# Regrouping the gated convolution's weights and starting its taps tile pair by tile pair, in a two-block transformer kernel

## The chip, the cores and the metric

The kernel runs on one core of one Trainium2 chip. TensorE (PE) multiplies, VectorE (DVE) and ScalarE (ACT) prepare its operands and take its results, SyncE issues the weight transfers. The metric is the device time in microseconds of one execution, as the median of three.

## What is computed

Two blocks over a sequence of 256 tokens with 2048 channels, all in float32. The first block (attention with a recurrence, then an MLP) is not touched. The second has two layers of this form, and the change is in these:

```python
z = h @ w_in[l]
q_lat, kv_lat, k_rope, mla_gate, conv_in, conv_gate = jnp.split(z, splits, axis=-1)   # 512, 256, 64, 1024, 2048, 1024
q = (rms_norm(q_lat, q_lat_g[l]) @ w_q_up[l]).reshape(b, s, N_HEADS, QK_DIM)
kv = (rms_norm(kv_lat, kv_lat_g[l]) @ w_kv_up[l])
...   # attention over 8 heads
mla_out = attn * jax.nn.silu(mla_gate)
u_val, u_gate = jnp.split(conv_in + glu_b[l], 2, axis=-1)
u = u_val * jax.nn.sigmoid(u_gate)                       # 1024 channels
u = causal_depthwise_conv(u, dw_w[l], dw_b[l])           # 31 taps per channel
u = jax.nn.silu(layer_norm(u, conv_ln_g[l], conv_ln_b[l]))
conv_out = (u @ w_pw[l] + b_pw[l]) * jax.nn.silu(conv_gate)
y = jnp.concatenate([mla_out, conv_out], axis=-1) @ w_out[l]
x = x + gate * y
```

## The kernel before

**Weights.** A float32 product is made of three products of rounded parts: high x high, high x low, low x high. Weights come from memory into four raw buffers (RAW). They are cut in *halves*, pieces of at most 1024 columns; for each half ACT writes the high part (WH, line 1922), DVE subtracts and writes the low part (WL, line 1084, called a split here), and PE multiplies both. There are four buffers of each part (`NHL = 4`), so ACT can make the high part of half j only when PE has finished half j - 4 (a wait on the semaphore `half_done`), and a DVE that is behind has at most that reserve before PE waits for it.

**Groups.** The weight columns are taken in groups, in an order written out by hand in `weight_course`. In a layer: 512 gates of the convolution (channel tiles 0 to 3), 256 + 256 of its values, 384 columns of key and value latents, 512 of query latents, the up-projection of the key and value latents (`w_kv_up`, four groups of one half), the other 512 gates, the other 512 values, the up-projection of the query latents (`w_q_up`, three groups of two halves), the gates of the attention (2 x 512) and of the convolution's output (4 x 256), then the halves of `w_out2` and `w_pw`. The two layers have the same program. I number the halves of a layer from 0: the first gates are halves 0 to 7, the query latents 24 to 31, the second gates 36 to 43, the second values 44 to 51, `w_q_up` 52 to 57.

**Two forms of product.** `products` multiplies each 128-column tile of weights in three matmuls of 256 columns (lines 578 to 580). `joint_products` is used for groups in `LAYER_JOINT`: the high weights go once against high and low hidden state side by side (512 columns, line 630), and the low weights against the high state (256 columns, line 632); ACT then takes the second half of the PSUM bank and DVE adds the first.

**PSUM pairs.** Each group is summed in a pair of PSUM banks. Groups in one pair follow each other: `n.before` is the mark (semaphore and value) that says that the pair's last group was taken out, and PE waits for it before the next group's first matmul:

```python
        if n.before:
            pe.wait_ge(*n.before)
```

For the second values of the convolution the mark is `taken`. DVE gives it after `glued` has taken the values out of PSUM, added the bias and multiplied by the gates (line 1820, four instructions of 256 columns, UV<-PS,PK,UG).

**Strands.** Everything else (normalisation, heads, attention, convolution) is written as generators, one per engine, and each is moved on by one step, a *beat*, behind each half. After a beat `cut_ahead` issues the next split, that of half j + 4 behind half j. So each engine's order is fixed: body of half j, beat j, split of half j + 4. `begin` hands out the halves; what stands in its loop body comes ahead of the beat. The convolution's taps are such a strand: tap 0 of a channel tile is an ACT instruction (line 2142), taps 1 to 30 are DVE instructions (line 1443, UG<-UV,PK,UG), 4 in a beat, 3 in the first `SLOW_TURNS` = 20. The first four channel tiles start behind half 15, the other four behind half 51. `channel_norm` starts when both are through.

Of the kernel before, what the change touches and what calls it, by code (L numbers as in the profile page):

```python
# [28 lines left out]
GLU_VALUES, GLU_GATES, Q_LATENT, KV_LATENT, MLA_GATES, CONV_GATES = ((0, 1), 5), (2, 6), 3, 4, (7, 8), (9, 10, 11, 12)  # L29
LAYER_JOINT = GLU_VALUES[0] + CONV_GATES  # L30
# [70 lines left out]
def weight_groups():  # L101

    return {
        "w_in": (16, [256] * 13 + [512] * 2 + [256] * 4),
        "w_out": (16, [512] * 4),
        "w_up": (16, [256] * 32),
        "w_down": (32, [512] * 8),
        "w_in2": (16, [256] * 2 + [512] * 2 + [384] + [512] * 4 + [256] * 4),
        "w_q_up": (4, [512] * 3),
        "w_kv_up": (2, [512] * 4),  # L110
        "w_pw": (8, [512] * 2),
        "w_out2": (16, [512] * 4),
    }
# [41 lines left out]
class Course:  # L155
# [84 lines left out]
def weight_course(t):  # L240
# [111 lines left out]
    "n_sum n_part n_mean n_sub n_sq n_ss n_ms n_root n_scale n_silu p_h p_l pw g_mm g_col g_out g_row g_mul x2"  # L352
# [124 lines left out]
def tensor_program(e, m, signals, plan):  # L477
# [451 lines left out]
    def channel_norm(L, taps):  # L929
# [3 lines left out]
        for n in range(15):  # L933
            if n == 0:
                b = small()
                pe.wait_ge("taps0", 124 * L + 124)
                pe.wait_ge("taps1", 124 * L + 124)
                spread_sum(b, lambda i: UG[:, i, :]).then_inc(signals["n_sum"], 1)
                free[b] = ("n_part", 2 * L + 1)
# [77 lines left out]
    for L in range(2):  # L1017
# [6 lines left out]
        products(group[f"w_in2_{L}", GLU_GATES[0]], *hidden, h, cols=4, early=h_early(2 + L))  # L1024
        course.pace = 99
        for g in GLU_VALUES[0]:
            joint_products(group[f"w_in2_{L}", g], h)
        taps = [course.start(convolution(L, 0))]
        products(group[f"w_in2_{L}", KV_LATENT], *hidden, h, cols=3)
        side_k = course.start(key_latents(L))  # L1030
        products(group[f"w_in2_{L}", Q_LATENT], *hidden, h, cols=4)
# [17 lines left out]
        for g in CONV_GATES:  # L1049
            joint_products(group[f"w_in2_{L}", g], h)  # L1050
        mla = tile_of("OH"), tile_of("OL"), lambda kt: ("o_l", 4 * L + kt // 2 + 1)
# [16 lines left out]
def vector_program(e, m, signals, plan):  # L1068
# [365 lines left out]
    def convolution(L, c0):  # L1434
        UV, UG = m["UV"], m["UG"]
        dw = pk(f"dw_w{L}").rearrange("p (c j) -> p c j", j=31)
        name = f"taps{c0 // 4}"
        for turn_ in course.tap_steps(L, c0):
            for n in turn_:
                j, c = n // 4, c0 + n % 4  # L1440
                if j:
                    dve.wait_ge(name, 124 * L + n - 3)
                    e.scalar_tensor_tensor(UG[:, c, :], UV[:, c, j:j + 256], dw[:, c, j:j + 1], UG[:, c, :], ALU.mult,  # L1443
                                           ALU.add).then_inc(signals[name], 1)
# [133 lines left out]
    def channel_norm(L, taps):  # L1578
# [3 lines left out]
        for n in range(15):  # L1582
            if n in (0, 2, 6, 8):
# [197 lines left out]
    for L in range(2):  # L1781
# [23 lines left out]
        def gated(c0):  # L1805

            dve.wait_ge(*group[f"w_in2_{L}", GLU_GATES[0]].taken)
            dve.wait_ge("joint_sum", 2 * joint_index(c0 // 2, L) + 2)
            tt("glu", UV[:, c0:c0 + 2, 30:286], UV[:, c0:c0 + 2, 30:286], UG[:, c0:c0 + 2, :], ALU.mult)

        def glued(g, c0):
            n = group[f"w_in2_{L}", g]
            for j, _ in course.begin(n):
                if j < n.done - 1:
                    continue
                dve.wait_ge("half_done", n.done)
                dve.wait_ge("uz", L + 1)
                dve.wait_ge(*group[f"w_in2_{L}", GLU_GATES[1]].taken)
                for f in range(4):
                    op = e.scalar_tensor_tensor(m["UV"][:, c0 + f, 30:286],  # L1820
                                                bank[2 * n.pair + f // 2][:, 256 * (f % 2):256 * (f % 2) + 256],
                                                pk(f"glu_b{L}")[:, c0 + f:c0 + f + 1], m["UG"][:, c0 + f, :], ALU.add,
                                                ALU.mult)
                op.then_inc(signals["taken"], 1)

        course.pace = 1
        course.group(group[f"w_in2_{L}", GLU_GATES[0]])
        course.pace = 99
        a, b = GLU_VALUES[0]
        course.group(group[f"w_in2_{L}", a])  # L1830
        n = group[f"w_in2_{L}", b]
        for j, _ in course.begin(n):
            if j == n.first + 1:
                summed(a, UV[:, 0:2, 30:286])
                gated(0)
            if j == n.done - 1:
                summed(b, UV[:, 2:4, 30:286])
                gated(2)
        taps = [course.start(convolution(L, 0))]
        course.group(group[f"w_in2_{L}", KV_LATENT])  # L1840
        side_k = course.start(key_latents(L))
        course.group(group[f"w_in2_{L}", Q_LATENT])
# [6 lines left out]
        course.group(group[f"w_in2_{L}", GLU_GATES[1]])  # L1849
        glued(GLU_VALUES[1], 4)  # L1850
        taps.append(course.start(convolution(L, 4)))
        norm = course.start(channel_norm(L, taps))
        course.drain(side_q)
        for g in range(3):
            course.group(group[f"w_q_up_{L}", g])
        flags.add(("queries", L))
        before = None
        for n in [group[f"w_in2_{L}", g] for g in MLA_GATES + CONV_GATES] + [
# [5 lines left out]
            before = next((g for g in CONV_GATES if group[f"w_in2_{L}", g] is n), None)  # L1864
        course.drain(side, norm)
# [44 lines left out]
def scalar_program(e, m, signals, plan, t):  # L1910
# [222 lines left out]
    def convolution(L, c0):  # L2133
        UV, UG = m["UV"], m["UG"]
        dw = pk(f"dw_w{L}").rearrange("p (c j) -> p c j", j=31)
        for turn_ in course.tap_steps(L, c0):
            for c in range(c0, c0 + 4) if turn_[0] == 0 else ():
                if c0:
                    act.wait_ge(*group[f"w_in2_{L}", GLU_VALUES[1]].taken)
                else:  # L2140
                    act.wait_ge("glu", 2 * L + c // 2 + 1)
                e.activation(UG[:, c, :], UV[:, c, 0:256], ACT.Identity, scale=dw[:, c, 0:1],
                             bias=pk(f"dw_b{L}")[:, c:c + 1]).then_inc(signals[f"taps{c0 // 4}"], 1)
# [20 lines left out]
    def query_latents(L):  # L2164
        QL, R2 = m["QN"][:, 0:4, :], m["R2"]
        for n in range(6):
            if n == 0:
                act.wait_ge(*group[f"w_in2_{L}", Q_LATENT].taken)
# [94 lines left out]
    def channel_norm(L, taps):  # L2263
# [3 lines left out]
        for n in range(15):  # L2267
            if n == 1:
# [46 lines left out]
    def store_R(n, dst):  # L2315
# [3 lines left out]
        op.then_inc(signals["stored"], 1)  # L2319

    def store_biased(n, dst, func, bias):
        act.wait_ge("half_done", n.done)
        for f in range(4):
            op = e.activation(dst(f), bank[2 * n.pair + f // 2][:, 256 * (f % 2):256 * (f % 2) + 256], func,
                              bias=bias[:, f:f + 1])
# [224 lines left out]
    for L in range(2):  # L2550
# [9 lines left out]
        def conv_gate(g, f0):  # L2560
            n = group[f"w_in2_{L}", g]
            course.group(n)
            store_biased(n, lambda f: UG[:, f0 + f, :], ACT.Sigmoid, glu[:, 8 + f0:12 + f0])
# [10 lines left out]
        conv_gate(GLU_GATES[0], 0)  # L2574
        course.pace = 99
        for c0, g in zip((0, 2), GLU_VALUES[0]):
            n = group[f"w_in2_{L}", g]
            for j, _ in course.begin(n):
                if j == n.done - 1:
# [241 lines left out]
```

## Time and profile before

| | |
|---|---|
| time, median of 3 (lowest to highest) | 1962.79 us (1962.68 to 1963.76) |
| the profiled execution's own time | 1963.59 us |
| its span, first to last instruction | 1961.8 us |
| PE busy | 1939.5 us, 99% |
| DVE busy | 1525.5 us, 78% |
| ACT busy | 1069.1 us, 54% |
| granted TensorE clock | 1.000 |

The two layers stand at about 1135 to 1541 us and 1545 us to the end of the span. A busy share says how long an engine had something to do, and not whether what it did was what the next one waited for; that is read from the waits and from the order of the instructions in time.

### The profile page before, as it was taken

The numbers are of one execution on the slowest core, as the hardware profiler recorded it, in microseconds if no ns is written. First come the engines' busy times: TensorE is split into PE (matmuls) and PEld (weight loads), VectorE is DVE, ScalarE is ACT, GpSimd is POOL, SyncE is SP. The second block draws the span as 40 slices with busy tenths as digits, with TensorE's granted clock in tenths as the row PEclk, the third lists the DMA queues.
The fourth block names the chain that finished last, engine by engine and source line by source line (L and its number), as shares of the span: only waits on it lengthen the run. The fifth ranks groups of instructions, "written<-read, shape, count | busy, mean of one in ns | idle before, by whom it ended". The sixth has DMA issues, their size and how long they took to land.

```text
span 1961.8 us, 27925 instructions
## 1 busy us (share of the span) xinstructions
PE 1939.5 (99%) x11546; PEld 1683.0 (86%) x11546; DVE 1525.5 (78%) x2092; ACT 1069.1 (54%) x1545; POOL 0.2 (0%) x4
## 2 busy tenths in 40 slices
PE   7999999999999999999999999999999999999999
PEld 6888888888888888888888889999888899998887
DVE  6587776868887777888877567999966669999764
ACT  5474766465664433555543475554764566456742
POOL 0000000000000000000000000000000000000000
PEclk9999999999999999999999999999999999999999
DMA  7443445938889888989898734544455455454453
GB/s 283 153 164 124 139 151 200 358 134 296 332 337 335 331 332 331 340 321 338 330 334 331 254 125 165 187 168 139 163 188 181 147 193 173 151 172 135 172 194 123
DMA packets 63982, 442.59 MB, mean 226 GB/s; under 512 B 7248, under 2 KB 7536, under 8 KB 12400
## 3 DMA queue, kind: packets, MB, share of 16 engines
q1 hardware_dynamic: 61920, 434.30, 61.9%
q10 hardware_dynamic: 1936, 6.51, 1.0%
q8 instruction: 91, 1.49, 0.3%
q14 instruction: 35, 0.29, 0.0%
HBM read 438.67 MB, written 2.11 MB: 225 GB/s over the span
## 4 chain that ended last, share of the span: by engine, by line
PE 96%; DVE 2%; ACT 1%; DMA 0%; issue 0%; ACTq 0%; DVEq 0%
PE PS L630 22%; PE PS L632 11%; PE PS L509 11%; PE PS L511 11%; PE PS L510 11%; PE PS L578 7%; PE PS L579 7%; PE PS L580 7%; PE PS L501 6%; PE PS L657 1%; DMA X<-in_x 0%; DVE WL L1084 0%; DVE Y L1126 0%; ACT S L1985 0%; ACT WH L1922 0%
## 5 line engine op out<-in xcount | busy, mean ns | idle before, releaser
L1922 ACT ACTIVATE WH<-RAW 128x1024 fp32r<-128x1024 f32 (+1 forms) x636 | 663.6, 1049 | 752.3 <-PE PS L511 282.5
L1084 DVE TENSOR_TENSOR WL<-RAW,WH 128x1024 fp32r<-128x1024 f32 (+1 forms) x636 | 766.4, 1209 | 374.7 <-ACT WH L1922 373.4
L630 PE MATMUL PS<-HT,WH 128*128 128x512 f32 x1912 | 678.5, 398 | 0.0
L632 PE MATMUL PS<-HT,WL 128*128 128x256 f32 x1912 | 535.8, 280 | 0.0
L630 PEld LDWEIGHTS PS<-HT,WH 128*128 128x128 f32 x1912 | 358.6, 188 | 88.8 <-issue 7.2
L632 PEld LDWEIGHTS PS<-HT,WL 128*128 128x128 f32 x1912 | 361.3, 189 | 0.1
L578 PE MATMUL PS<-HT,WH 128*128 128x256 f32 x1008 | 291.2, 289 | 0.7 <-DVE HT L1135 0.4
L580 PE MATMUL PS<-HT,WL 128*128 128x256 f32 x1008 | 285.5, 283 | 0.0
L579 PE MATMUL PS<-HT,WH 128*128 128x256 f32 x1008 | 285.5, 283 | 0.0
L1093 DVE SCALAR_TENSOR_TENSOR RAW<-RAW,CB 128x2048 f32<-128x2048 f32 x96 | 219.3, 2284 | 0.0
L511 PE MATMUL PS<-WH,Ul 128*128 128x512 f32 x512 | 203.0, 396 | 0.0
L509 PE MATMUL PS<-WH,Uh 128*128 128x512 f32 x512 | 202.5, 396 | 0.0
L578 PEld LDWEIGHTS PS<-HT,WH 128*128 128x128 f32 x1008 | 193.4, 192 | 10.6 <-issue 7.8
L510 PE MATMUL PS<-WL,Uh 128*128 128x512 f32 x512 | 201.2, 393 | 0.0
L1443 DVE SCALAR_TENSOR_TENSOR UG<-UV,PK,UG 128x256 f32<-128x256 f32 x480 | 200.4, 478 | 0.2
L579 PEld LDWEIGHTS PS<-HT,WH 128*128 128x128 f32 x1008 | 193.6, 192 | 0.4
L580 PEld LDWEIGHTS PS<-HT,WL 128*128 128x128 f32 x1008 | 193.5, 192 | 0.0
L510 PEld LDWEIGHTS PS<-WL,Uh 128*128 128x128 f32 x512 | 96.1, 188 | 23.8
L511 PEld LDWEIGHTS PS<-WH,Ul 128*128 128x128 f32 x512 | 96.1, 188 | 23.7
L509 PEld LDWEIGHTS PS<-WH,Uh 128*128 128x128 f32 x512 | 96.1, 188 | 22.5
L509 PE MATMUL PS<-WH,HT 128*128 128x512 f32 x256 | 100.8, 394 | 0.0
L511 PE MATMUL PS<-WH,HT 128*128 128x512 f32 x256 | 99.8, 390 | 0.0
(317 smaller groups left out, 2026.7 us busy)
## 6 DMA issues: line engine op xcount, KB each, us to landing
RAW<-in_w_in SPq DMA_DIRECT2D x112, 1024.0 KB, 4.8
RAW<-in_ada_w SPq DMA_DIRECT2D x96, 1024.0 KB, 6.3
RAW<-in_w_up SPq DMA_DIRECT2D x64, 1024.0 KB, 5.8
RAW<-in_w_down SPq DMA_DIRECT2D x64, 1024.0 KB, 5.7
RAW<-in_w_out SPq DMA_DIRECT2D x48, 1024.0 KB, 4.8
RAW<-in_w_pw SPq DMA_DIRECT2D x8, 1024.0 KB, 4.8
RAW<-in_w_in SPq DMA_DIRECT2D x8, 768.0 KB, 4.2
RAW<-in_w_q_up SPq DMA_DIRECT2D x6, 1024.0 KB, 4.8
```

The costliest lines, as they stand in the source:

```text
L509: e.matmul(out, sh, mh, start=st, stop=False, skip_group_check=True)
L510: e.matmul(out, sh, ml, start=False, stop=False, skip_group_check=True)
L511: return e.matmul(out, sl, mh, start=False, stop=final, skip_group_check=True)
L578: e.matmul(out, sh, ah, start=first and i % 2 == 0, stop=False, skip_group_check=True)
L579: e.matmul(out, sh, al, start=False, stop=False, skip_group_check=True)
L580: op = e.matmul(out, sl, ah, start=False, stop=final, skip_group_check=True)
L630: e.matmul(bk[i][:, 0:512], wh[:, at], m["HT"][:, kt, :, :].rearrange("p a t -> p (a t)"), start=kt == 0, stop=False, skip_group_check=True)
L632: op = e.matmul(bk[i][:, 0:256], wl[:, at], HTh[:, kt, :], start=False, stop=kt == n.kts - 1, skip_group_check=True)
L1084: e.tensor_tensor(m[f"WL{j % NHL}"][:, 0:nk * w], m[f"RAW{i % NRAW}"][:, k0 * w:(k0 + nk) * w], m[f"WH{j % NHL}"][:, 0:nk * w].bitcast(F32 ...
L1093: e.scalar_tensor_tensor(raw[:, :], raw[:, :], 1.0, m["CB"][:, :], ALU.mult, ALU.mult, accum_out=mod[:, k:k + 1]).then_inc(signals["ada"], 1)
L1443: e.scalar_tensor_tensor(UG[:, c, :], UV[:, c, j:j + 256], dw[:, c, j:j + 1], UG[:, c, :], ALU.mult, ALU.add).then_inc(signals[name], 1)
L1922: e.activation(m[f"WH{j % NHL}"][:, 0:nk * w], m[f"RAW{i % NRAW}"][:, k0 * w:(k0 + nk) * w], ACT.Copy).then_inc(signals["high"], 1)
```

## The change

The convolution's gates and values of the same two channel tiles now come in one weight group: of 512 columns, 256 gates and 256 values. There are three such groups (`GLU`, for tiles 0 and 1, 4 and 5, 6 and 7), multiplied by `products`; tiles 2 and 3 come in two groups of 256 (`GLU_JOINT`, gates then values), multiplied by `joint_products`. The query latents are two groups of 256 with `joint_products`. The number of halves in a layer and their places stay the same. The taps start behind half 7 and behind half 43, and first only on one pair of channel tiles; the other pair joins in at a later turn. The multiplication by the gates is done pair by pair. The last steps of `channel_norm` wait for a flag that is set when all of `w_in2` has been multiplied.

```diff
-GLU_VALUES, GLU_GATES, Q_LATENT, KV_LATENT, MLA_GATES, CONV_GATES = ((0, 1), 5), (2, 6), 3, 4, (7, 8), (9, 10, 11, 12)
-LAYER_JOINT = GLU_VALUES[0] + CONV_GATES
+GLU, GLU_JOINT, Q_LATENT, KV_LATENT, MLA_GATES, CONV_GATES = (0, 6, 7), (1, 2), (3, 4), 5, (8, 9), (10, 11, 12, 13)
+LAYER_JOINT = GLU_JOINT + Q_LATENT + CONV_GATES
...
     def tap_steps(self, L, c0):
-        yield range(4)
-        n, turn = 4, 0
-        while n < 124:
-            k = min(3 if c0 == 0 and turn < SLOW_TURNS else 4, 124 - n)
-            yield range(n, n + k)
-            n, turn = n + k, turn + 1
+        later = 7 if c0 == 0 else 10
+        done = [0] * 4
+        for turn in range(99):
+            taps = []
+            if turn in (1, later):
+                taps = [(0, c0 + c) for c in ((0, 1) if turn == 1 else (2, 3))]
+            for _ in range(3 if c0 == 0 and later < turn <= later + SLOW_TURNS else 4):
+                c = min(range(4 if turn > later else 2), key=lambda c: done[c])
+                if turn > 1 and done[c] < 30:
+                    done[c] += 1
+                    taps.append((done[c], c0 + c))
+            yield taps
+            if sum(done) == 120:
+                return
...
-        weights(f"w_in2_{layer}", (GLU_GATES[0], *GLU_VALUES[0], KV_LATENT, Q_LATENT))
+        weights(f"w_in2_{layer}", (GLU[0], *GLU_JOINT, KV_LATENT, *Q_LATENT))
         weights(f"w_kv_up_{layer}", range(4))
-        weights(f"w_in2_{layer}", (GLU_GATES[1], GLU_VALUES[1]))
+        weights(f"w_in2_{layer}", GLU[1:])
...
-            elif tensor[:4] == "w_pw" or tensor[:5] == "w_in2" and g == GLU_VALUES[1]:
+            elif tensor[:4] == "w_pw" or tensor[:5] == "w_in2" and g in GLU:
                 taken += 1
                 mark = ("taken", taken)
```

In PE's program:

```diff
-        for g in (GLU_GATES[1], GLU_VALUES[1]):
-            products(group[f"w_in2_{L}", g], *hidden, h, cols=4)
+        products(group[f"w_in2_{L}", GLU[1]], *hidden, h, cols=4)
         taps.append(course.start(convolution(L, 4)))
+        products(group[f"w_in2_{L}", GLU[2]], *hidden, h, cols=4)
```

In DVE's program:

```diff
+        def glued(g, c0, gates):
             n = group[f"w_in2_{L}", g]
+            dve.wait_ge("half_done", n.done)
+            dve.wait_ge("uz", L + 1)
+            dve.wait_ge("u_sig", 4 * L + gates)
+            for c in range(c0, c0 + 2):
+                op = e.scalar_tensor_tensor(UV[:, c, 30:286], bank[2 * n.pair + 1][:, 256 * (c - c0):256 * (c - c0) + 256],
+                                            pk(f"glu_b{L}")[:, c:c + 1], UG[:, c, :], ALU.add, ALU.mult)
+            op.then_inc(signals["taken"], 1)
...
-        course.group(group[f"w_in2_{L}", GLU_GATES[1]])
-        glued(GLU_VALUES[1], 4)
+        course.group(group[f"w_in2_{L}", GLU[1]])
         taps.append(course.start(convolution(L, 4)))
+        n = group[f"w_in2_{L}", GLU[2]]
+        for j, _ in course.begin(n):
+            if j == n.first + 1:
+                glued(GLU[1], 4, 3)
         norm = course.start(channel_norm(L, taps))
         course.drain(side_q)
         for g in range(3):
-            course.group(group[f"w_q_up_{L}", g])
+            n = group[f"w_q_up_{L}", g]
+            for j, _ in course.begin(n):
+                if g == 0 and j == n.first + 1:
+                    glued(GLU[2], 6, 4)
```

In ACT's program, tap 0 of a channel tile:

```diff
-            for c in range(c0, c0 + 4) if turn_[0] == 0 else ():
-                if c0:
-                    act.wait_ge(*group[f"w_in2_{L}", GLU_VALUES[1]].taken)
+            for j, c in turn_:
+                if j:
+                    continue
+                if c in (2, 3):
+                    act.wait_ge("glu", L + 1)
                 else:
-                    act.wait_ge("glu", 2 * L + c // 2 + 1)
+                    act.wait_ge(*group[f"w_in2_{L}", GLU[(c + 2) // 4 if c else 0]].taken)
```

**DVE around `w_q_up`, layer 0.** L1084 (before) and L1097 (changed) are the splits, L1443 and L1462 the taps, L1820 and L1839 the multiplication of PSUM values by the gates, whose last instruction gives `taken`. Before, from the split of half 53:

```order
L1084 TENSOR_TENSOR WL<-RAW,WH 128x1024 [waits high]
L1443 SCALAR_TENSOR_TENSOR UG<-UV,PK,UG 128x256 [waits taps0] x4
L1084 TENSOR_TENSOR WL<-RAW,WH 128x1024 [waits high]
L1820 SCALAR_TENSOR_TENSOR UV<-PS,PK,UG 128x256 [waits stored,uz,half_done]
L1820 SCALAR_TENSOR_TENSOR UV<-PS,PK,UG 128x256 x3
L1443 SCALAR_TENSOR_TENSOR UG<-UV,PK,UG 128x256 [waits taps0] x4
L1084 TENSOR_TENSOR WL<-RAW,WH 128x1024 [waits high] x2
L1443 SCALAR_TENSOR_TENSOR UG<-UV,PK,UG 128x256 [waits taps1] x4
```

In the changed kernel, from the same split:

```order
L1097 TENSOR_TENSOR WL<-RAW,WH 128x1024 [waits high]
L1462 SCALAR_TENSOR_TENSOR UG<-UV,PK,UG 128x256 [waits taps1] x4
L1097 TENSOR_TENSOR WL<-RAW,WH 128x1024 [waits high]
L1462 SCALAR_TENSOR_TENSOR UG<-UV,PK,UG 128x256 [waits taps1] x4
L1097 TENSOR_TENSOR WL<-RAW,WH 128x1024 [waits high]
L1462 SCALAR_TENSOR_TENSOR UG<-UV,PK,UG 128x256 [waits taps1] x4
L1097 TENSOR_TENSOR WL<-RAW,WH 128x1024 [waits high]
L1839 SCALAR_TENSOR_TENSOR UV<-PS,PK,UG 128x256 [waits u_sig,half_done]
L1839 SCALAR_TENSOR_TENSOR UV<-PS,PK,UG 128x256
L1462 SCALAR_TENSOR_TENSOR UG<-UV,PK,UG 128x256 [waits taps1] x4
```

The instructions that give `taken` stood behind the split of half 54 and now stand behind that of half 56, with two more splits and eight taps ahead of them; there are two of them in place of four (two others moved ahead, into the body of half 45).

**PE at the second group of `w_q_up`.** QLh and QLl are the query latents' parts. Before:

```order
L578 MATMUL PS<-QLh,WH 128x256
L579 MATMUL PS<-QLl,WH 128x256
L580 MATMUL PS<-QLh,WL 128x256
L578 MATMUL PS<-QLh,WH 128x256 [waits split,taken]
L579 MATMUL PS<-QLl,WH 128x256
```

In the changed kernel:

```order
L587 MATMUL PS<-QLh,WH 128x256
L588 MATMUL PS<-QLl,WH 128x256
L589 MATMUL PS<-QLh,WL 128x256
L587 MATMUL PS<-QLh,WH 128x256 [waits split,taken]
L588 MATMUL PS<-QLl,WH 128x256
```

The wait stands at the same place, the first matmul of half 54, and for the same mark; what has to be done on DVE before the mark is given has moved, as shown above.

## Rows read from the trace of the kernel before

**Rows 1.** The page, busy time of each engine and the clock by slices.

```profile
PE 1939.5 (99%) x11546; PEld 1683.0 (86%) x11546; DVE 1525.5 (78%) x2092; ACT 1069.1 (54%) x1545; POOL 0.2 (0%) x4
...
PEclk9999999999999999999999999999999999999999
```

**Rows 2.** Waits of PE over the whole span: us in total, times, longest.

```profile
PE PS L657 <- DVE Y L1126: 14.0, 3, 12.3
PE PS L501 <- DVE Y L1080: 1.6, 1, 1.6
PE PS L564 <- ACT VT L1965: 1.5, 2, 0.9
```

**Rows 3.** Windows: length, busy time of PE, PEld, DVE, ACT, POOL, then clock.

```profile
12.30:18.20 5.90, 5.65 (x24) 4.93 (x24) 5.88 (x14) 3.75 (x9) 0.00 (x0) 1.00 1.01 361
...
1160.00:1541.00 381.00, 381.00 (x2604) 343.92 (x2603) 313.04 (x519) 215.08 (x314) 0.00 (x0) 1.00 0.50 171
...
1565.00:1957.00 392.00, 392.00 (x2669) 353.66 (x2668) 317.07 (x523) 213.63 (x306) 0.00 (x0) 1.00 0.49 166
```

**Rows 4.** PE's timeline, a plain group and a joint group: start, us, instruction.

```profile
1200.16 0.28 PE L578 MATMUL PS<-HT,WH 128*128 128x256 f32 x1
...
1201.60 0.28 PE L578 MATMUL PS<-HT,WH 128*128 128x256 f32 x1
...
1189.20 0.39 PE L630 MATMUL PS<-HT,WH 128*128 128x512 f32 x1
...
1190.24 0.39 PE L630 MATMUL PS<-HT,WH 128*128 128x512 f32 x1
```

**Rows 5.** PE's timeline, first matmul of half 52 and of half 54; half 52, layer 1.

```profile
1300.69 0.28 PE L578 MATMUL PS<-QLh,WH 128*128 128x256 f32 x1
...
1306.45 0.28 PE L578 MATMUL PS<-QLh,WH 128*128 128x256 f32 x1
...
1709.41 0.28 PE L578 MATMUL PS<-QLh,WH 128*128 128x256 f32 x1
```

**Rows 6.** DVE's timeline, splits of halves 53 to 56, in brackets idle before.

```profile
1298.49 1.67 DVE L1443 SCALAR_TENSOR_TENSOR UG<-UV,PK,UG 128x256 f32<-128x256 f32 x4
1300.08 1.22 DVE L1084 TENSOR_TENSOR WL<-RAW,WH 128x1024 fp32r<-128x1024 f32 x1
1301.21 1.67 DVE L1443 SCALAR_TENSOR_TENSOR UG<-UV,PK,UG 128x256 f32<-128x256 f32 x4
1302.80 1.22 DVE L1084 TENSOR_TENSOR WL<-RAW,WH 128x1024 fp32r<-128x1024 f32 x1
1304.05 1.66 DVE L1820 SCALAR_TENSOR_TENSOR UV<-PS,PK,UG 128x256 f32<-128x256 f32 x4
1305.62 1.67 DVE L1443 SCALAR_TENSOR_TENSOR UG<-UV,PK,UG 128x256 f32<-128x256 f32 x4
```

**Rows 7.** The same, layer 1.

```profile
1712.77 1.66 DVE L1820 SCALAR_TENSOR_TENSOR UV<-PS,PK,UG 128x256 f32<-128x256 f32 x4
```

**Rows 8.** DVE's timeline before that: last wait, and splits of halves 48 and 49.

```profile
1267.12 1.23 DVE L1084 TENSOR_TENSOR WL<-RAW,WH 128x1024 fp32r<-128x1024 f32 x1 [0.32 <-ACT WH L1922]
...
1283.14 1.23 DVE L1084 TENSOR_TENSOR WL<-RAW,WH 128x1024 fp32r<-128x1024 f32 x1
1284.29 1.67 DVE L1443 SCALAR_TENSOR_TENSOR UG<-UV,PK,UG 128x256 f32<-128x256 f32 x4
1285.99 0.75 DVE L1525 SCALAR_TENSOR_TENSOR KN<-KN,PK,PS 128x512 f32<-128x512 f32 x1
1286.65 0.84 DVE L1528 TENSOR_TENSOR KP<-KV,PS 64x256 f32<-64x256 f32 x2
1287.53 1.23 DVE L1084 TENSOR_TENSOR WL<-RAW,WH 128x1024 fp32r<-128x1024 f32 x1
```

**Rows 9.** ACT's timeline: a high part, tap 0 of four tiles, two high parts.

```profile
1300.89 1.06 ACT L1922 ACTIVATE WH<-RAW 128x1024 fp32r<-128x1024 f32 x1 [1.76 <-PE PS L580]
1305.74 2.08 ACT L2142 ACTIVATE UG<-UV,PK 128x256 f32<-128x256 f32 x4 [3.79 <-DVE UV L1820]
1307.73 1.99 ACT L1922 ACTIVATE WH<-RAW 128x1024 fp32r<-128x1024 f32 x2
```

**Rows 10.** DVE's timeline, key and value latents: DVE without a wait.

```profile
1198.56 0.96 DVE L1084 TENSOR_TENSOR WL<-RAW,WH 128x768 fp32r<-128x768 f32 x1 [1.41 <-ACT WH L1922]
1199.44 1.27 DVE L1443 SCALAR_TENSOR_TENSOR UG<-UV,PK,UG 128x256 f32<-128x256 f32 x3
1200.63 0.95 DVE L1084 TENSOR_TENSOR WL<-RAW,WH 128x768 fp32r<-128x768 f32 x1
```

More of the change, by code:

```diff
@@ L1437, in convolution @@
         name = f"taps{c0 // 4}"
+        n, last = 120 * L, {}
         for turn_ in course.tap_steps(L, c0):
[L1439 to L1444, printed above, removed]
+            for j, c in turn_:
+                if not j:
+                    continue
+                if j == 1:
+                    dve.wait_ge("taps_a", 8 * L + c + 1)
+                else:
+                    dve.wait_ge(name, last[c])
+                n += 1
+                last[c] = n
+                e.scalar_tensor_tensor(UG[:, c, :], UV[:, c, j:j + 256], dw[:, c, j:j + 1], UG[:, c, :], ALU.mult,
+                                       ALU.add).then_inc(signals[name], 1)
             yield
@@ L1582, in channel_norm @@
         for n in range(15):
+            while n == 10 and ("inputs", L) not in flags:
+                yield
             if n in (0, 2, 6, 8):
@@ L1803, in summed, with gated @@
                 tt("joint_sum", part[:, i, :], bank[2 * n.pair + i][:, 0:256], part[:, i, :], ALU.add)
[L1805 to L1811, printed above, removed]
-            n = group[f"w_in2_{L}", g]
[L1813 to L1824, printed above, removed]
+        def gated():
+            dve.wait_ge("u_sig", 4 * L + 2)
+            dve.wait_ge("joint_sum", 2 * joint_index(GLU_JOINT[1], L) + 2)
+            tt("glu", UV[:, 2:4, 30:286], UV[:, 2:4, 30:286], UG[:, 2:4, :], ALU.mult)
@@ L1826, in vector_program @@
         course.pace = 1
-        course.group(group[f"w_in2_{L}", GLU_GATES[0]])
+        course.group(group[f"w_in2_{L}", GLU[0]])
         course.pace = 99
-        a, b = GLU_VALUES[0]
+        taps = [course.start(convolution(L, 0))]
+        a, b = GLU_JOINT
+        n = group[f"w_in2_{L}", a]
+        for j, _ in course.begin(n):
+            if j == n.first + 1:
+                glued(GLU[0], 0, 1)
+        n = group[f"w_in2_{L}", b]
+        for j, _ in course.begin(n):
+            if j == n.first + 1:
+                summed(a, UG[:, 2:4, :])
+            if j == n.done - 1:
+                summed(b, UV[:, 2:4, 30:286])
+                gated()
@@ L1830, in vector_program @@
+        course.group(group[f"w_in2_{L}", KV_LATENT])
+        side_k = course.start(key_latents(L))
+        a, b = Q_LATENT
         course.group(group[f"w_in2_{L}", a])
@@ L1833, in vector_program @@
             if j == n.first + 1:
-                summed(a, UV[:, 0:2, 30:286])
-                gated(0)
+                summed(a, m["QN"][:, 0:2, :])
             if j == n.done - 1:
[L1837 to L1842, printed above, removed]
+                summed(b, m["QN"][:, 2:4, :])
         side_q = course.start(query_latents(L))
@@ L2167, in query_latents @@
             if n == 0:
[L2168 removed]
+                act.wait_ge("joint_sum", 2 * joint_index(Q_LATENT[1], L) + 2)
                 act.wait_ge("l_ss", 2 * L + 1)
@@ L2267, in channel_norm @@
         for n in range(15):
+            while n == 10 and ("inputs", L) not in flags:
+                yield
             if n == 1:
@@ L2558, in scalar_program, with gate_pair @@
         glu = pk(f"glu_b{L}")
-        def conv_gate(g, f0):
+        def gate_pair(g, c0):
             n = group[f"w_in2_{L}", g]
-            course.group(n)
-            store_biased(n, lambda f: UG[:, f0 + f, :], ACT.Sigmoid, glu[:, 8 + f0:12 + f0])
+            act.wait_ge("half_done", n.done)
+            for c in range(c0, c0 + 2):
+                op = e.activation(UG[:, c, :], bank[2 * n.pair][:, 256 * (c - c0):256 * (c - c0) + 256], ACT.Sigmoid,
+                                  bias=glu[:, 8 + c:9 + c])
+            op.then_inc(signals["u_sig"], 1)
         def second_part(n, part, func=ACT.Copy, bias=None):
```

75 lines of the change are left out of this document (47 added, 28 removed).

## The prediction

> **What bounds the kernel now.** I start from the page: PE has something to do in 99% of the span and the granted clock is full in all slices [rows 1], so only two things can change the time: PE's own work, and a wait put in front of it. Then the waits of PE [rows 2]. There are three of any size, 12.3 us of the largest at the kernel's start and the rest at the borders between stages. Inside the layers there is none, and the windows say the same without inference: in the 381 us from 1160 to 1541 PE is busy for 381.00, in the 392 us from 1565 to 1957 for 392.00 [rows 3]. So nothing that makes DVE or ACT quicker in the layers can be worth anything, and starting the taps earlier, which moves work off the end of a layer, is worth nothing by itself. The question is only whether DVE still delivers in time. It is busy for 313.04 of those 381 us [rows 3], which is not an idle engine, and what matters is how far it is behind at each place where PE needs it.
>
> That is read from DVE's timeline. Its last wait before `w_q_up` is at 1267.12, on ACT [rows 8]. From there it has more to do per half than PE. A turn of four taps and a split take 2.72 us from start to start (1300.08 to 1302.80 [rows 6]); a half of PE takes 2.88 us (1300.69 to 1306.45 for two [rows 5]). With the heads' instructions a turn takes 4.39 us (1283.14 to 1287.53 [rows 8]). So DVE falls behind by about 1.5 us in each of several halves, and wins back only 0.16 us in each after. PE does not notice, since four halves of split weights lie in reserve. At 1302.80 DVE starts the split of half 54 [rows 6], which PE starts at 1306.45 [rows 5]: the split is ready at 1304.02, 2.4 us early, where the reserve at full depth would be some 6 us. DVE lags, harmlessly, because splits are asked for four halves ahead. A result that PE asks for one half ahead does not have this reserve.
>
> **The change part by part.**
>
> *Query latents with a joint operand.* In a plain group twelve matmuls take 1200.16 to 1201.60, 0.360 us for each three; in a joint group three pairs take 1189.20 to 1190.24, 0.347 us each [rows 4]. Three matmuls and one pair do the same work, a 128-column weight tile in one of 16 row tiles. Four such tiles by 16 are 64 units a layer: 64 x 0.013 = 0.83 us, 1.7 us in two layers. This is the whole change in PE's work. The gates and values of tiles 0 to 7 change places but not form: 512 of their columns were joint before and 512 are now.
>
> *DVE's and ACT's work.* The joint latents cost DVE four additions a layer; the gating loses one multiplication of 512 columns. The taps are the same 240 a layer. None is on PE's path while the reserve holds.
>
> *The wait that is moved.* In a layer the PSUM pair of `w_q_up`'s second group (half 54) is the one that held the convolution's last values, before and now, and PE waits there for `taken`. Before, DVE took these values in the body of half 51, behind the split of half 54: at 1304.05, four instructions, 1.66 us, over at 1305.71 [rows 6]. PE came at 1306.45 [rows 5]: early by 0.74 us, with nothing to spare for more. Now they are taken in the body of half 53, behind the split of half 56 (the order above). Step by step, from the split of half 54 at 1302.80:
> - two turns of four taps and a split, 2.72 us each [rows 6], bring DVE to the start of the split of half 56: 1308.24;
> - from a split to this gating, 1.25 us (1302.80 to 1304.05): 1309.49;
> - four gating instructions take 1.57 us to the next start and 1.66 to their end; so two take 0.39 + 0.48 = 0.87: over at 1310.36.
>
> PE is there at 1306.45. It waits 3.9 us. The joint latents bring PE there 0.8 us sooner, but DVE as well, whose splits follow PE through `half_done` up to 1267.12; I count that gain once, above.
>
> Does DVE reach 1302.80 earlier than before? The turn behind half 44 is the same four taps, that behind half 45 has no tap (-1.59 us), and two gating instructions come ahead of it (+0.79): 0.8 us less. But tap 0 of two tiles is now done by ACT in that turn and waits for this gating. The split of half 48 ends at 1284.37 [rows 8], the gating at 1285.24, two tap-0 instructions take half of 2.08 us [rows 9], the high part of half 49 takes 1.06: 1287.34, and the split of half 49, at 1287.53 before, can start at about 1287.4. Of the 0.8 us some 0.1 stays. I take 3.8 us; if all of the 0.8 stayed it would be 3.1, and with a longer chain through ACT 4.2.
>
> The second layer is the same program: half 52 starts there at 1709.41 and the gating at 1712.77 [rows 5, 7], both 408.72 us after the first, so it waits as long: 7.6 us in two layers. What is queued behind the wait on PE is all the rest of the layer, and since PE waits for nothing else in it, there is no idle time later in which this comes back. ACT's tap 0 of tiles 6 and 7 waits for the same mark, with the high part of half 58 behind it; PE reaches that half four halves later, so it costs nothing. DVE, in return, is no longer behind after the stall, which no one needs.
>
> *Small waits.* A joint half is 0.1 us shorter, and DVE gets 24 taps into halves 10 to 15, so chains between small matmuls and DVE are tighter. Nothing in the trace shows such a wait; between 0 and 0.4 us a layer, I take 0.1.
>
> **Sum.** 1963.59 (the profiled execution; span 1961.8) - 1.7 + 7.6 + 0.2 = 1969.7. That execution was 0.8 us above the median of the runs, 1962.79, so for the median: 1962.79 + 6.1 = **1968.9 us**. Its own range, from 3.1 to 4.2 a layer and 0 to 0.4 for small waits: 1967.3 to 1970.3.
>
> **The clock.** The largest pause of PE in the layers before is nil, and that before them under 2 us [rows 2], and the clock is granted in full throughout [rows 3]. A pause of 3.8 us is longer than any inside the span after the start, so no row says that the clock survives it. If it falls to the lower of its two levels (1.2 for 2.4 GHz), PE works at half speed for a time that no row gives; bounded by the pause itself it would be up to 3.8 us at half speed, 1.9 us lost for each stall. The Trainium skill ("TensorE: Matmul & The Clock Gate", the table on what matters for kernels) says that idle gaps between bursts put the clock back to its lower level; by it each of the two stalls would cost more than its own length. No run so far shows it.
>
> **The rivals.**
> - *The mark is given in time* (not slower). If DVE were not behind, the gating in half 53's body would still stand behind that half's predecessor split, and come 1.06 (high part) + 1.25 + 0.87 = 3.2 us after half 52's end at 1303.57, at 1306.75: a wait of 0.3 us. This needs DVE to have won back the 3.6 us by which it is behind. It decides from there: each us of lag on DVE is one on PE. Against it is that the same 2.72 us turns run through halves 46 to 53 in both. Time: 1962.79 - 1.7 + 0.6, 1961.7, within what tells from no change. Chance 0.06.
> - *Half of it*: the ACT chain spares more, or DVE's turns are shorter with other neighbours; 1.9 us a layer, 1965.1. Chance 0.06.
> - *The clock falls* in one or both pauses: 1970.8 or 1972.7. Chance 0.17.
> - *Splits late as well*: in the key and value latents PE has halves of 2.16 us and DVE three taps and a split in 2.07 (1198.56 to 1200.63 [rows 10]), so a delay from halves 8 to 15 stays. DVE's work there rises from none to 4 taps in six halves (2.72 of 2.78 us) and gating; it starts the stage 1 to 2 us later than before, against a reserve of over 3. If it fails, PE waits for another 1 us a layer: 1970.9. Chance 0.05.
> - The forecast itself: 0.66.
>
> **How the numbers follow.** A measurement of this kernel tells about 0.2%, 3.9 us, from no change. Slower by more than that: the forecast, the late splits and the clock, 0.88. The in-time case and the half of it are within: 0.12, of which I give 0.02 to faster, for a gain that I don't see (PE's work alone gives only 1.7 us). The range leaves out those two cases below and the fall of the clock in both pauses above: 1966.3 to 1971.5.
>
> **What would show it.** Right: a wait of PE at the first matmul of `w_q_up`'s second group, line 587, released by DVE's line 1839, two times, some 3.8 us each; PE's busy time in the layers otherwise 0.8 us less each; DVE without a pause for ACT from half 49 to the gating; joint pairs at 0.347 us in halves 24 to 31. Wrong: no such wait, or one under 2 us; a granted clock under 1 behind it; new waits for line 1097 in the key and value latents.

## The result and the profile after

The changed kernel takes 1973.97 us (median of 4, 1972.90 to 1974.22), the kernel before 1962.85: ratio 1.0054, 95% interval 1.0041 to 1.0066. It is slower, as forecast, but by 11.1 us in place of 6.1, and outside the range of 1966.3 to 1971.5.

The page of the changed kernel, span, busy times and the clock by slices, to be held against [rows 1]:

```profile
span 1971.1 us, 27683 instructions
PE 1940.2 (98%) x11418; PEld 1678.6 (85%) x11418; DVE 1528.8 (78%) x2102; ACT 1068.0 (54%) x1549; POOL 0.2 (0%) x4
...
PEclk9999999999999999999999999999999999999999
```

With 128 matmuls fewer PE has more busy time, and the page's clock row shows nothing, since a digit stands for 49 us. The line of the cores does: span and mean granted clock.

```profile
core 0: 1971.1 us, clock 0.998
```

The three largest waits of PE over the whole span (us in total, times, longest), against [rows 2]:

```profile
PE PS L666 <- DVE Y L1139: 14.0, 3, 12.3
PE PS L587 <- DVE UV L1839: 7.6, 2, 3.8
PE PS L510 <- DVE Y L1093: 1.6, 1, 1.6
```

The middle row is new, and it is the forecast one: first matmul of half 54, released by the gating, twice, 3.8 us each. DVE's timeline up to it, against [rows 6] (the split of half 54 is that at 1301.50):

```profile
1301.50 1.22 DVE L1097 TENSOR_TENSOR WL<-RAW,WH 128x1024 fp32r<-128x1024 f32 x1
1302.64 1.67 DVE L1462 SCALAR_TENSOR_TENSOR UG<-UV,PK,UG 128x256 f32<-128x256 f32 x4
1304.22 1.22 DVE L1097 TENSOR_TENSOR WL<-RAW,WH 128x1024 fp32r<-128x1024 f32 x1
1305.36 1.67 DVE L1462 SCALAR_TENSOR_TENSOR UG<-UV,PK,UG 128x256 f32<-128x256 f32 x4
1306.94 1.22 DVE L1097 TENSOR_TENSOR WL<-RAW,WH 128x1024 fp32r<-128x1024 f32 x1
1308.19 0.88 DVE L1839 SCALAR_TENSOR_TENSOR UV<-PS,PK,UG 128x256 f32<-128x256 f32 x2
```

The gating ends 1308.19 + 0.88 - 1301.50 = 7.57 us after the start of the split of half 54; the prediction had 1310.36 - 1302.80 = 7.56. Both PE and DVE come here 1.3 us earlier than before: 0.4 us of it is the joint latents, 0.9 us the first block, whose program is unchanged (see the last section). What the prediction left out of its likeliest case is what PE does next. PE's timeline at the wait:

```profile
1305.02 0.28 PE L589 MATMUL PS<-QLh,WL 128*128 128x256 f32 x1
1309.12 0.38 PE L587 MATMUL PS<-QLh,WH 128*128 128x256 f32 x1 [3.82 <-DVE UV L1839]
...
1309.60 0.41 PE L587 MATMUL PS<-QLh,WH 128*128 128x256 f32 x1
1309.81 0.41 PE L588 MATMUL PS<-QLl,WH 128*128 128x256 f32 x1
1310.02 0.41 PE L589 MATMUL PS<-QLh,WL 128*128 128x256 f32 x1
```

Behind the pause a matmul follows the last after 0.21 us, where it took 0.12 [rows 5]. The windows of the changed kernel (length, busy time of PE with its matmuls, PEld, DVE, ACT, POOL, then the granted clock) show why:

```profile
1297.00:1304.00 7.00, 7.00 (x61) 7.00 (x60) 7.00 (x15) 3.68 (x5) 0.00 (x0) 1.00 0.66 247
1304.00:1309.00 5.00, 1.31 (x11) 1.09 (x10) 4.97 (x10) 2.03 (x3) 0.00 (x0) 1.00 0.49 177
1309.00:1313.50 4.50, 4.38 (x24) 4.38 (x25) 4.37 (x10) 1.09 (x2) 0.00 (x0) 0.62 0.33 76
1313.50:1317.00 3.50, 3.50 (x32) 3.50 (x31) 2.07 (x4) 1.41 (x2) 0.00 (x0) 1.00 0.62 262
...
1723.00:1727.50 4.50, 4.50 (x26) 4.50 (x27) 4.24 (x9) 1.06 (x2) 0.00 (x0) 0.67 0.27 56
```

In the 4.5 us behind the pause the mean clock is 0.62, which is the lower level (1.2 GHz, half) for 0.38 / 0.5 x 4.5 = 3.4 us and the higher one for the rest; in layer 1 it is 0.67, so 3.0 us at the lower level lie in this window. PE counts as busy all the while.

### The profile page after: what moved, and what is told of

It reads as the page before. It is cut to its first block, busy times and chain, and to the rows that moved or that the text cites. A ratio compares the mean times of both kernels' runs of the same rounds, so it can differ in the third digit from the quotient of the medians.

```text
span 1971.1 us, 27683 instructions
## 1 busy us (share of the span) xinstructions
PE 1940.2 (98%) x11418; PEld 1678.6 (85%) x11418; DVE 1528.8 (78%) x2102; ACT 1068.0 (54%) x1549; POOL 0.2 (0%) x4
## 4 chain that ended last, share of the span: by engine, by line
PE 83%; DVE 14%; ACT 2%; issue 1%; DMA 0%; ACTq 0%; DVEq 0%
PE PS L639 22%; PE PS L520 11%; PE PS L518 11%; PE PS L519 11%; PE PS L641 11%; PE PS L510 5%; DVE UG L1462 5%; DVE WL L1097 5%; PE PS L587 4%; PE PS L588 4%; PE PS L589 4%; ACT WH L1956 1%; PE PS L666 1%; DMA X<-in_x 0%; DVE Y L1139 0%
## 5 line engine op out<-in xcount | busy, mean ns | idle before, releaser
L1097 DVE TENSOR_TENSOR WL<-RAW,WH 128x1024 fp32r<-128x1024 f32 (+1 forms) x636 | 766.3, 1209 | 383.7 <-ACT WH L1956 382.0
L639 PE MATMUL PS<-HT,WH 128*128 128x512 f32 x2040 | 723.2, 398 | 0.1
L639 PEld LDWEIGHTS PS<-HT,WH 128*128 128x128 f32 x2040 | 382.5, 188 | 95.2 <-issue 7.4
L587 PE MATMUL PS<-HT,WH 128*128 128x256 f32 x880 | 254.5, 289 | 1.6 <-DVE HT L1148 1.3
L588 PE MATMUL PS<-HT,WH 128*128 128x256 f32 x880 | 249.0, 283 | 0.0
L1462 DVE SCALAR_TENSOR_TENSOR UG<-UV,PK,UG 128x256 f32<-128x256 f32 x480 | 200.7, 479 | 0.3
L587 PEld LDWEIGHTS PS<-HT,WH 128*128 128x128 f32 x880 | 168.7, 192 | 11.2 <-issue 7.2
L588 PEld LDWEIGHTS PS<-HT,WH 128*128 128x128 f32 x880 | 169.0, 192 | 0.3
L518 PEld LDWEIGHTS PS<-WH,Uh 128*128 128x128 f32 x512 | 96.1, 188 | 22.5
```

Of the source, the lines that this page charges most:

```text
L518: e.matmul(out, sh, mh, start=st, stop=False, skip_group_check=True)
L587: e.matmul(out, sh, ah, start=first and i % 2 == 0, stop=False, skip_group_check=True)
L588: e.matmul(out, sh, al, start=False, stop=False, skip_group_check=True)
L639: e.matmul(bk[i][:, 0:512], wh[:, at], m["HT"][:, kt, :, :].rearrange("p a t -> p (a t)"), start=kt == 0, stop=False, skip_group_check=True)
L1097: e.tensor_tensor(m[f"WL{j % NHL}"][:, 0:nk * w], m[f"RAW{i % NRAW}"][:, k0 * w:(k0 + nk) * w], m[f"WH{j % NHL}"][:, 0:nk * w].bitcast(F32 ...
```

## The experiments

I call a stretch of 3.4 us at half clock a spell. One takes 3.4 x 0.5 / 1972 = 0.0009 off the mean clock of a whole execution, so 0.999, 0.998 and 0.997 are read as one, two and three spells. The traces show one (e4_move_alone) or two (the changed kernel, twice); three are read from a mean of 0.997 alone. Each run is compared with runs of the kernel before on the same chip (medians 1962.83 us for e1_early, e2_warm, e3_short and e4_move_alone, 1963.69 for a2_again, e5_fewer_taps, e6_joint_alone and e7_norm_late, 1962.90 for e8_joint_only).

To compare a stage between runs I use the first and last start of PE's matmuls on the query latents, line 578 or 587, `w_q_up`, halves 52 to 57. Before, they go from 1300.7 to 1317.6, 16.9 us.

**e1_early: the late gating put back by two halves, from the body of half 53 to that of half 51.** In DVE's program:

```diff
             if j == n.first + 1:
                 glued(GLU[1], 4, 3)
+            if j == n.done - 1:
+                glued(GLU[2], 6, 4)
...
-                if g == 0 and j == n.first + 1:
-                    glued(GLU[2], 6, 4)
```

In ACT's program:

```diff
-        course.group(group[f"w_in2_{L}", GLU[2]])
-        gate_pair(GLU[2], 6)
+        for j, _ in course.begin(group[f"w_in2_{L}", GLU[2]]):
+            if j == group[f"w_in2_{L}", GLU[2]].done - 1:
+                gate_pair(GLU[2], 6)
```

> The changed kernel with one thing moved: the last two gating instructions (tiles 6 and 7), which give the mark for the second group of w_q_up, stand in the body of half 51, on DVE and on ACT, in place of half 53. Theory (DVE's lag reaches PE through this mark alone, and the pause then lowers the clock): no wait for it, clock 1.000, only the joint latents are left, so 1.7 us under before: 1961.2 us. Rival (the time went to splits that come late because taps and gating lie in other halves): little changes, 1970 us or more. Rival (only the wait counts and the clock's fall is by chance): 1961 to 1963 as well, so this run does not tell it from the theory.

Measured: 1963.38 us, ratio 1.0002 (0.9993 to 1.0011), clock 1.000. The wait for line 1839 is gone from PE's waits; this one call, moved, takes away 10.6 us between the medians and 9.5 us between the spans of the profiled executions (1971.1 and 1961.6). But 1961.2 was expected, and of the gain by the joint latents nothing is to be seen. PE's timeline in the first group of query latents of this kernel, three pairs of the joint form:

```profile
1214.06 0.40 PE L639 MATMUL PS<-HT,WH 128*128 128x512 f32 x1
...
1215.12 0.40 PE L639 MATMUL PS<-HT,WH 128*128 128x512 f32 x1
```

1.06 us, 0.353 for a pair, where [rows 4] had 0.347 in halves 8 to 15 of the same form: half of the expected gain. And a wait that the kernel before does not have, in its waits of PE:

```profile
PE PS L510 <- DVE HS L1536: 0.4, 2, 0.2
```

**e2_warm: the wait filled with matmuls that nobody needs.**

```diff
         for g in range(3):
+            if g == 1:
+                keep_warm(16)
             products(group[f"w_q_up_{L}", g], tile_of("QLh"), tile_of("QLl"), lambda kt: ("l_l", 2 * L + 2), cols=4)
```

> The changed kernel with 16 matmuls of 128 columns on constants, whose results nobody uses, put on PE ahead of the wait at the second group of w_q_up. By the trace of before such a matmul takes 0.223 us, so they fill 3.6 of the 3.9 us. The wait's end is set by DVE and stays. Theory (a pause of PE lowers the clock for 3.4 us, which costs 1.4 us in each layer, seen in the profile): clock 1.000, span 2.8 us under the changed kernel's 1971.1, median 1969 to 1970. Rival (the low clock in the profile is not caused by the pause): clock stays 0.998, 1973 to 1974 us.

Measured: 1970.11 us (1970.03 to 1970.17), ratio 1.0036 (1.0024 to 1.0049), clock 1.000. The windows of this kernel at the same place:

```profile
1304.00:1309.00 5.00, 4.93 (x44) 4.74 (x42) 4.97 (x10) 2.03 (x3) 0.00 (x0) 1.00 0.53 172
1309.00:1313.50 4.50, 4.37 (x36) 4.38 (x37) 4.41 (x11) 2.15 (x3) 0.00 (x0) 1.00 0.30 78
```

The added matmuls fill the wait but for 0.2 us (the trace has two instructions for each of the 16):

```profile
1305.19 3.73 PE L510 MATMUL PS<-CN 128*128 128x128 f32 x32
1309.13 0.39 PE L587 MATMUL PS<-QLh,WH 128*128 128x256 f32 x1 [0.20 <-DVE UV L1841]
```

Behind the filled wait 36 matmuls fit into the 4.5 us, behind the empty one 24. The stage `w_q_up` takes from 1299.4 to 1320.4, 21.0 us, in the changed kernel 1299.4 to 1321.9, 22.5 us. So the pause itself costs 21.0 - 16.9 = 4.1 us and the clock 1.5 more. In layer 1 the same stage takes 16.9 us before, 20.9 here and 22.2 in the changed kernel: 4.0 for the pause, 1.3 for the clock. Together the clock costs 2.8 us in the profiled executions, which is also the difference of their spans, 1971.1 - 1968.3.

The medians are 3.9 us apart, 1.0 more. No trace shows where this 1.0 lies. A third spell does not explain it: of the changed kernel's four executions only the one at 1974.22 us had a mean clock of 0.997, while 1973.91 and 1974.04 had 0.998, like the profiled one at 1972.90. What fits is the first block, which takes 0.9 us more in some executions than in others (last section): it took the shorter time in both profiles, and the five executions of e2_warm lie within 0.1 us of its profiled one.

**e3_short: the late gating one half earlier.**

```diff
-                if g == 0 and j == n.first + 1:
+                if g == 0 and j == n.first:
                     glued(GLU[2], 6, 4)
```

> The changed kernel with the last gating moved one half ahead, from the body of half 53 to that of half 52. On DVE one turn of taps and split, 2.72 us, is no longer ahead of it. Theory: PE waits 3.8 - 2.7 = 1.1 us in each layer, the clock does not fall, so 1962.85 - 1.7 + 2.2 + 0.3 = 1963.7 us. Rival (any wait at this place lowers the clock): 2.8 us more, 1966.5 us.

Measured: 1964.71 us, ratio 1.0010 (1.0001 to 1.0019), clock 1.000. The wait, in its waits of PE:

```profile
PE PS L587 <- DVE UV L1839: 2.1, 2, 1.1
```

One turn of taps and split less ahead of the gating is 2.7 us less for PE to wait, and a pause of 1.1 us did not lower the clock in any of the eleven executions. The median is 1.0 us above the expectation, where the run with the early gating was 2.2 above: both counted 1.7 us for the joint latents, which bring only half of it (e8_joint_only below).

**e4_move_alone: the kernel before with only the gating of tiles 4 to 7 moved to the body of half 53.** The taps of these tiles and channel_norm start behind it.

```diff
-            for j, _ in course.begin(n):
-                if j < n.done - 1:
-                    continue
...
         for g in range(3):
-            course.group(group[f"w_q_up_{L}", g])
+            for j, _ in course.begin(group[f"w_q_up_{L}", g]):
+                if g == 0 and j == group[f"w_q_up_{L}", 0].first + 1:
+                    glued(GLU_VALUES[1], 4)
+            if g == 0:
+                taps.append(course.start(convolution(L, 4)))
+                norm = course.start(channel_norm(L, taps))
```

> The kernel before with one thing alone: its gating of tiles 4 to 7 is done in the body of half 53 in place of half 51, and the taps of these tiles start behind it. No joint latents, no regrouping, no early taps. Theory (the place of the mark on DVE's queue is the cause): DVE has a turn of taps less in between than the changed kernel, and four gating instructions, so the mark comes at 1309.5 in the time of before, PE waits 3.1 us in each layer; 1962.85 + 6.2 = 1969 us with the clock kept, 1971.9 if it falls in both. Rival (the regrouping and the early taps put DVE behind): no wait or one under 1 us, 1963 to 1965 us.

Measured: 1972.22 us (1970.62 to 1973.97), ratio 1.0049 (1.0035 to 1.0063). Without any of the regrouping almost the whole loss is there. Its waits of PE, and two of its windows behind the pause, layer 0 and layer 1:

```profile
PE PS L578 <- DVE UV L1818: 6.0, 2, 3.0
...
1309.00:1313.50 4.50, 4.50 (x39) 4.50 (x39) 1.25 (x2) 2.92 (x5) 0.00 (x0) 1.00 0.83 299
...
1717.00:1723.00 6.00, 3.00 (x17) 2.79 (x16) 4.79 (x7) 4.10 (x7) 0.00 (x0) 0.80 0.63 187
```

In this execution a pause of 3.0 us left the clock alone in layer 0 and lowered it in layer 1: a pause of that length can go either way. The five executions had mean clocks 0.999, 0.998, 0.998, 0.998, 0.997 and took 1970.62, 1971.85, 1972.27, 1972.22, 1973.97 us. Read as one, two and three spells, that is some 1.6 us each; only the first of them was traced.

**a2_again: the changed kernel once more.** No edit.

> The changed kernel as it is, once more, to see how the fall of the clock varies from one execution to the next. If each pause lowers the clock for one spell of 3.4 us, all runs lie at 1972.9 to 1974.2 with a mean clock of 0.998. If a pause can lower it for two spells, some runs show 0.997 or 0.996 and lie 1.5 us or more above the others. The waits themselves should not vary.

Measured: 1974.88 us (1973.10 to 1975.74), ratio 1.0055 (1.0043 to 1.0068). The clocks were 0.998, 0.998, 0.997, 0.998, 0.997 with 1973.2, 1973.1, 1975.1, 1975.74, 1974.88 us. The waits are again 7.6, 2, 3.8 in the profiled execution, the one at 1973.2 us with two spells. Two executions at 0.997 point to a third spell; neither was traced, so whether a third pause went with it isn't seen. One run at 0.998 took 1975.74, so not all of the spread is the clock's.

**e5_fewer_taps: seven taps less ahead of the late gating.**

```diff
-            for _ in range(3 if c0 == 0 and later < turn <= later + SLOW_TURNS else 4):
+            for _ in range(3 if c0 == 0 and later < turn <= later + SLOW_TURNS or c0 and turn <= 8 else 4):
```

> The changed kernel with three taps in place of four in turns 2 to 8 of the second convolution strand (behind halves 46 to 52), so 7 taps of 0.4 us less ahead of the late gating, made up by two more turns at the end. The mark stays where the change put it. Theory (the wait is as long as DVE's lag): the wait shrinks by 2.8 us to about 1.0 us in each layer, the clock stays, 1964.7 us as with the gating one half ahead. Rival (the wait is set by the place alone, by ACT's or PE's chain): still near 3.8 us and 1973 us.

Measured: 1965.58 us (1964.67 to 1967.70), ratio 1.0012 (1.0003 to 1.0021), clock 1.000. The mark stands where the change put it, and its row in the waits of PE is:

```profile
PE PS L587 <- DVE UV L1839: 2.1, 2, 1.0
```

The wait is DVE's lag: 2.8 us less work ahead of the gating, 2.8 us less wait. The eleven executions spread over 3.0 us at a full clock; the slower ones were not traced.

**e6_joint_alone: the query latents in the joint form, on the kernel before.** In this build the gates and values of channel tiles 4 to 7 are exchanged (the sizes and the work are the same), which the next run sets right.

```diff
-LAYER_JOINT = GLU_VALUES[0] + CONV_GATES
+LAYER_JOINT = GLU_VALUES[0] + Q_LATENT + CONV_GATES
...
-        products(group[f"w_in2_{L}", Q_LATENT], *hidden, h, cols=4)
+        for g in Q_LATENT:
+            joint_products(group[f"w_in2_{L}", g], h)
```

> The kernel before with the query latents in two groups with the joint form, and nothing else of the change. Forecast of the prediction: 1.7 us less, 1961.2 us. By the profiles of the changed kernel and of the one with early gating, where halves 24 to 31 took only 0.42 us less than before: 0.84 us less, 1962.0 us. If the small loss behind half 56 (0.7 us a layer) came with the joint latents and not with the earlier channel_norm, 1963.4 us.

Measured: 1962.88 us beside 1963.69 for the kernel before, ratio 0.9997 (0.9988 to 1.0006).

**e8_joint_only: the same with all of the computation in place.**

> The kernel before with the query latents in the joint form as its only change, all of the computation in place. By the run of the same form with gates and values of four channel tiles exchanged: halves 24 to 31 take 0.42 us less in each layer and nothing else moves, 0.85 us less in all, ratio 0.9996. Forecast of the prediction for this part: 1.7 us less, ratio 0.9991.

Measured: 1962.05 us beside 1962.90, 0.85 us less, ratio 0.9996 (0.9987 to 1.0005). That is the expectation by halves 24 to 31 and half of what the prediction had. It is the lowest median of the study, though the interval does not exclude no change.

**e7_norm_late: e1_early with channel_norm held back.** In all three programs:

```diff
         while any(strand in course.strands for strand in taps):
             yield
+        for _ in range(7):
+            yield
```

> The changed kernel with the early gating (1963.38 us), and channel_norm held back by seven turns, so that its steps fall on the halves on which they fell before. Theory (in that kernel halves 56 to 98 take 0.7 us a layer more than before, of which 0.4 because channel_norm's matmuls cut in at other places): 0.8 us less, 1962.5 us. Rival (the 0.4 comes from elsewhere): 1963.4 us.

Measured: 1963.51 us, ratio 0.9999 (0.9990 to 1.0008), on the chip whose median of before is 1963.69; e1_early was 0.55 us above its median of before, this one is 0.18 below. The profile tells it better, in the time from the first `w_q_up` matmul to the last start of a matmul on the attention's output (OH), half 97, in layer 0. The rows of e7_norm_late (duration min/median/max, then first and last start):

```profile
L587 PE MATMUL PS<-QLh,WH x48: 278/280/283, 1302.0 to 1318.9; 128*128 128x256 f32 x48
L518 PE MATMUL PS<-WH,OH x32: 392/397/582, 1438.2 to 1460.5; 128*128 128x512 f32 x32
```

and of e1_early:

```profile
L587 PE MATMUL PS<-QLh,WH x48: 278/280/283, 1299.5 to 1316.4; 128*128 128x256 f32 x48
L518 PE MATMUL PS<-WH,OH x32: 392/397/400, 1436.6 to 1458.4; 128*128 128x512 f32 x32
```

158.9 us in e1_early, 158.5 with channel_norm held back, and 158.2 both before (1300.7 to 1458.9) and in e8_joint_only (1299.6 to 1457.8). So an earlier channel_norm costs 0.4 us a layer, and 0.3 stay; the wait for the heads' reciprocal (HS), 0.2 in each layer, is most of that.

## Why the prediction was wrong

By its own steps:

- **What bounds the kernel**: right. PE was without a pause in the layers, so earlier taps brought nothing: e1_early, which has them without the wait, is 0.6 us above before.
- **The wait that is moved**: right in place, cause and size. 3.8 us forecast, 3.8 measured, in both layers. e3_short and e5_fewer_taps show that its length is DVE's lag (2.7 and 2.8 us less for one turn or seven taps less), e1_early that the place of the gating alone makes it, e4_move_alone that it needs nothing else of the change. Of the 0.8 us by which DVE might have come earlier nothing stayed, where 0.1 was forecast: it waited 0.69 us for ACT ahead of the split of half 49, at 1286.23, and from there to the gating for nothing. The stage loses 4.1 and 4.0 us by the pause, 0.2 to 0.3 more than the 3.8 of the sum.
- **Query latents with a joint operand**: right mechanism, twice too large. The term was 64 x 0.013 us a layer, from a pair at 0.347 us in halves 8 to 15. In halves 24 to 31 a pair takes 0.353, the term is 0.42 us a layer and 0.85 in all (e8_joint_only) in place of 1.7. I took the rate of the one place for that of the other.
- **Small waits**: 0.1 us a layer forecast, with 0.4 as the upper end. With the early gating it is 0.7 (e1_early), 0.4 of it from channel_norm's matmuls at other halves (e7_norm_late), which the prediction valued at nothing.
- **The clock**: this is the step that failed. The prediction put the clock's fall at nothing in its sum and kept it as a rival with a chance of 0.17. It wrote that "no row says that the clock survives it", and gave no reason for deciding that it does. In all nine executions of the changed kernel the mean clock was 0.998 or 0.997. e2_warm shows that the idle time of PE is the cause: with the mark given at the same time and PE kept at work, the clock stays, and the profiled execution is 2.8 us nearer to before (the median 3.9 us). The Trainium skill ("TensorE: Matmul & The Clock Gate", section "Why this matters for your kernels") says that idle gaps between matmul bursts throw the clock back to its lower level. The traces agree for the long pause: 0.62 of the clock behind 3.8 us, 1.00 behind 1.1, and either behind 3.0.
- **The price of the clock**: 1.9 us for each pause was the bound. A spell costs 1.5 us in layer 0 and 1.3 in layer 1 of the profiled executions. With both pauses the rival gave 1972.7 us; measured were 1973.97 and, on another chip, 1974.88 beside 1963.69.
- **A row that was misread**: the prediction says that the clock is granted in full throughout, by [rows 3]. The first window there has 1.00 as well, but 24 matmuls in 5.9 us where the next has 49. In the kernel before, PE's matmuls behind the idle 12.3 us at the start stand 0.21 us apart and last 0.41, as they do behind the pause here, and from 18.4 on they stand 0.12 apart:

```profile
14.99 0.41 PE L578 MATMUL PS<-HT,WH 128*128 128x256 f32 x1
15.21 0.41 PE L579 MATMUL PS<-HT,WH 128*128 128x256 f32 x1
...
18.82 0.28 PE L578 MATMUL PS<-HT,WH 128*128 128x256 f32 x1
18.93 0.28 PE L579 MATMUL PS<-HT,WH 128*128 128x256 f32 x1
```

So the column of the clock can't be trusted at the start of a span, and the one long idle stretch on record was followed by the lower pace. PE had done nothing before it, so it shows no fall; but it was the nearest row for a long pause, and it spoke for the rival.

The sum with the sizes as measured in the profiles: two pauses 4.1 + 4.0 = 8.1, clock 2.8, joint latents -0.85: 10.05 us. The spans differ by 1971.1 - 1961.8 = 9.3 us; but the profiled execution of the kernel before had the slower first block, by 0.9 us, which makes 10.2. The medians differ by 11.1. The 0.9 left over is the size of that same step of the first block, which would come in if most executions of the changed kernel had the slower one; there is no trace of them, so this is not shown.

The sum leaves nothing for channel_norm and the small waits, and the traces agree there. From the last `w_q_up` matmul on QLh in layer 0 to the first in layer 1 it is 391.6 us before, 391.8 in e1_early, but 391.2 in the changed kernel, e2_warm, e3_short and e5_fewer_taps; 0.4 less than before is what the joint latents of layer 1 bring. So where PE has waited for the gating, even for 1.1 us, the 0.7 us of e1_early are not lost. I take this for slack that DVE has after the wait; no run tests that reason.

What stays open: the last 0.9 us between the medians, whether and why a third spell comes in some executions, and why a pause of 3.0 us lowers the clock in one layer and not in the other. No run moved a pause of one length in time.

## What to carry to other kernels

When an instruction that frees a PSUM bank is moved past others on a busy engine, count from the engine's last idle moment to the new place, and compare with when PE comes: a result asked for one step ahead has none of the reserve that lets the same engine run late with work asked for four steps ahead. A pause of PE must be priced with the clock: ask whether it is longer than any the trace has survived, and if so put the fall into the likeliest sum. Read the clock also from the distance of equal matmuls, since its column can say 1.00 where they stand twice as far apart. If the pause can't be avoided, dummy matmuls in it give back the clock's part (here 2.8 us in the profiled executions), but moving the mark to an earlier place gives back nearly all of the loss (9.5 us).

## What the hardware showed unexpectedly

The joint form has two rates. A pair takes 0.347 us in some stretches and 0.353 in others. In the layers the place decides: halves 8 to 15 are fast and halves 24 to 31 slow in every profile. In the first block the same instructions go at either rate from one execution to the next; in the 40 us from 430 on, the row of line 632's matmuls in the kernel before is

```profile
430.00:470.00 40.00, 31.81 (x114) 21.40 (x114) 1.00 0.77 268
```

and in e6_joint_alone, whose first block is the same program,

```profile
430.00:470.00 40.00, 32.29 (x116) 21.85 (x116) 1.00 0.77 275
```

114 pairs and 116 in the same time at the same clock. That is 0.7 us over this stretch. Over the whole first block it is 0.9: this row of PE at its end, in the kernel before and in the changed one,

```profile
1138.65 5.18 PE L501 MATMUL PS<-CN 128*128 128x128 f32 x44 [1.57 <-DVE Y L1080]
...
1137.76 5.18 PE L510 MATMUL PS<-CN 128*128 128x128 f32 x44 [1.57 <-DVE Y L1093]
```

is the same instructions behind the same program. The executions of the kernel before do lie mostly in two groups about 0.9 us apart (1962.6 to 1963.2 and 1963.5 to 1963.8). So a difference of under 1 us between two single profiles, or between medians that can fall into either group, says nothing unless it is read stage by stage. What sets the rate is open.
